# A layer's first DeltaNet unit in another order: substitution ahead of query norm and decay product, masks on VectorE, three weight roundings on ScalarE, gate values in another PSUM bank

## The chip, the cores and the metric

The kernel runs on one core of a Trainium2 chip. The time is that of the whole program on the device, in microseconds (us). TensorE (PE) multiplies matrices into PSUM, VectorE (DVE), ScalarE (ACT) and GpSimd (POOL) work element by element, SyncE (SP) and ScalarE issue the DMA transfers used here. Each engine has one queue of instructions and runs it in order; between engines they wait on semaphores.

## What is computed

Two layers of a hybrid decoder trunk on a sequence of 1024 tokens, width 1024. Each layer projects the normalised input with one matrix of 9232 columns and feeds two branches: a retention branch (4 heads) and a gated DeltaNet branch (8 heads). The change is in the second one.

```python
def gated_deltanet(q, k, v, beta, g):            # chunks; k, q l2-normed after conv and SiLU
    gc = jnp.cumsum(g, axis=-1)                  # within a chunk
    decay = jnp.exp(jnp.where(causal, gc[..., :, None] - gc[..., None, :], -jnp.inf))
    L = jnp.where(strict, einsum(k_beta, k) * decay, 0.0)
    a = L + jnp.eye(C)
    sol = triangular_solve(a, [v * beta, k_beta * exp(gc)])   # lower, unit diagonal
    attn = einsum(q, k) * decay
    ...                                          # recurrence over the chunks
```

beta and g come from sixteen narrow columns of the same projection (the gates).

## The kernel before

**Dense products.** Every weight block is 1024 x 128 in float32. To keep precision it is split into a rounded part w_hi and the rest w_lo (the residual); the activations are split likewise, and each of a block's sixteen pieces is three products with 512 columns (lines 746, 748, 750). Blocks alternate between two slots of w_hi and w_lo. One buffer, w_raw, takes the block from memory, so the load of a block (`load_w`, line 570) waits for the residual of the block before it. The rounding is done by VectorE (`split_w`, line 1581) or, in the even and odd units, by ScalarE (`split_hi`, line 1264); the residual by VectorE (`low_w`, line 1587) in a layer's first unit and by GpSimd (line 2230) elsewhere.

**Units.** The DeltaNet work of a layer is cut into units of half a head, 512 tokens, four chunks of 128. While the recurrence of one half runs, the next half is prepared: gram products of the keys (`gram`, TensorE, line 961), their diagonal for the key norm (`diag`, `keys`), the masked decays (`mask`, line 2308 for the lower one and 2310 for the transposed one, both on GpSimd), their exponentials (`dec`, ScalarE, lines 1393 and 1398), the negated L (`nl`, VectorE, line 1891), the inverse of its 16 x 16 diagonal blocks by substitution (`solve`, thirty small VectorE operations, lines 1976 and 1979), its spread into the full matrix (`spread`, line 1986) and three doubling levels (`turn`, `level_v`, `level_x`), in which TensorE makes two groups of products per level (lines 998 or 1002, then 1013, 1015 or 1017) and VectorE copies or multiplies each result (lines 1946 or 1951, then 1959, 1962 or 1965). The queries are transposed and squared (`qt`), summed for their norm (`qe`, lines 1908 to 1914), and the query-key product (`kq`, TensorE line 978) is multiplied by the transposed decays on VectorE (line 1921).

**The diagonal blocks' way.** The substitution needs the diagonal blocks in another layout, and they go through memory: after `nl` they are stored with small transfers (SyncE line 630, in the first unit half of them ScalarE, line 1413), and when all have landed they are loaded (line 638, and ScalarE line 1423, which stands in its queue behind `kc`, a weight load and the evacuation of the V block's first half).

**The first unit.** A layer starts with a unit that has no recurrence beside it, only preparation of head 0's first half (step index 0) and the keys of its second half (index 1), over the pieces of four blocks Q, V, D, R. The order of all engines comes from one list, `unit_schedule(kind)`: 36 slots (`at(n, step)`), two pieces (`fill`) after the steps of each slot, and after the pieces convolution steps (`conv`), `tanh` and `silu`, none or one or two per slot. Each engine walks the list and issues its own part of each step. In the first unit the substitution starts in slot 17 and the spread is in slot 24. Ahead of the unit TensorE transposes the gate values into bank 3 (line 903), VectorE copies them (line 1752), and from them a chain over both engines makes g_tok (line 1762), the input of the cumulative sum (`gc`, line 941). Gram 0 writes bank 3 as well, and waits for that copy.

## Time and profile before

| | |
|---|---|
| median of 3 runs | 2701.21 us (2700.89 to 2704.86) |
| profiled execution | 2703.87 us, its span 2702.1 us |
| TensorE busy | 98% of the span |
| VectorE, ScalarE, GpSimd busy | 61%, 23%, 31% |
| mean granted TensorE clock | 0.998 |

The profile is one execution. A row of the timeline gives the start in us from the span's start, the time, engine, line and operation, and in brackets how long the engine was idle before it and what released it. Times of matrix products overlap, since they are pipelined. Many tiles of the kernel lie in one tensor called arena, so lines tell more than names.

### The profile page before, as it was taken

To read this page: it belongs to the slowest core of one execution; us is meant where nothing else is said; L and a number is where in the kernel's file an instruction comes from. 1 tells how busy PE (TensorE), PEld (TensorE's weight loads), DVE (VectorE), ACT (ScalarE), POOL (GpSimd) and SP (SyncE) were. 2 spreads that over 40 slices of the span, in tenths; PEclk is the share of its full clock that TensorE was granted. 3 is DMA by queue.
4 is the path that set the end of the run, shared out by engine and by line. 5 is a ranking of instruction groups with operands and counts; after the bars stand their busy time and mean duration, and the time that the engine had idled before them with its cause. 6 is when DMAs were issued, how large, how long until landed. Compare 5 with 4: busy or idle time off the path is not lost.

```text
span 2702.1 us, 39281 instructions
## 1 busy us (share of the span) xinstructions
PE 2654.9 (98%) x14674; PEld 2260.2 (84%) x14674; DVE 1647.2 (61%) x3718; ACT 626.2 (23%) x1261; POOL 836.1 (31%) x459
## 2 busy tenths in 40 slices
PE   7999999999999999999999999999999999999998
PEld 6888888888888888888878888888888888888886
DVE  7878777877744443434587778777877434443333
ACT  5333333333211101200142333333322111120001
POOL 3233333333321212434522333333332122232443
PEclk9999999999999999999999999999999999999999
DMA  4321222122211112433532222222222111133344
GB/s 169 95 87 52 84 63 87 52 84 64 83 42 39 48 35 70 124 100 116 157 95 81 74 78 61 74 73 80 60 78 65 42 49 42 40 107 98 94 140 140
DMA packets 292832, 217.79 MB, mean 81 GB/s; under 512 B 31682, under 2 KB 246036, under 8 KB 292388
## 3 DMA queue, kind: packets, MB, share of 16 engines
q1 hardware_dynamic: 254322, 151.21, 19.6%
q10 hardware_dynamic: 38322, 64.07, 7.1%
q8 instruction: 118, 1.93, 0.3%
q14 instruction: 70, 0.57, 0.1%
HBM read 176.37 MB, written 38.86 MB: 80 GB/s over the span
## 4 chain that ended last, share of the span: by engine, by line
PE 85%; DVE 7%; DMA 2%; POOL 2%; issue 2%; ACT 1%; SPq 1%; ACTq 0%; DVEq 0%; POOLq 0%
PE dense_ps L746 21%; PE dense_ps L750 20%; PE dense_ps L748 20%; PE work L729 3%; PE dense_ps L770 2%; PE dense_ps L771 2%; PE dense_ps L772 2%; PE work L1002 1%; DMA arena<-l_scratch 1%; PE work L961 1%; PE work L1039 1%; PE work L978 1%; PE work L1059 1%; PE work L1028 1%; PE work L1052 1%
## 5 line engine op out<-in xcount | busy, mean ns | idle before, releaser
L746 PE MATMUL dense_ps<-act_hi,w_hi 128*128 128x512 f32 x2560 | 1063.6, 415 | 6.2 <-DVE w_lo L2110 2.4
L750 PE MATMUL dense_ps<-act_hi,w_lo 128*128 128x512 f32 x2560 | 1002.5, 392 | 0.0
L748 PE MATMUL dense_ps<-act_lo,w_hi 128*128 128x512 f32 x2560 | 1000.1, 391 | 0.0
L2230 POOL TENSOR_TENSOR w_lo<-w_raw,w_hi 128x1024 fp32r<-128x1024 f32 x164 | 404.7, 2468 | 1072.1 <-ACT w_hi L1264 565.2
L750 PEld LDWEIGHTS dense_ps<-act_hi,w_lo 128*128 128x128 f32 x2560 | 480.6, 188 | 106.3
L746 PEld LDWEIGHTS dense_ps<-act_hi,w_hi 128*128 128x128 f32 x2560 | 482.9, 189 | 91.0 <-DVE w_lo L2110 2.9
L748 PEld LDWEIGHTS dense_ps<-act_lo,w_hi 128*128 128x128 f32 x2560 | 483.4, 189 | 81.6 <-issue 0.5
L1726 DVE SCALAR_TENSOR_TENSOR arena<-arena,cols 128x512 f32<-128x512 f32 x288 | 241.3, 838 | 5.1
L1581 DVE CAST w_hi<-w_raw 128x1024 fp32r<-128x1024 f32 x90 | 63.7, 708 | 187.8 <-PE dense_ps L772 112.7
L729 PE MATMUL work<-mk,arena 128*128 128x128 f32 x768 | 113.4, 277 | 13.3 <-issue 7.5
L1740 DVE SCALAR_TENSOR_TENSOR arena<-arena 128x512 f32<-128x512 f32 x96 | 112.8, 1175 | 13.2 <-ACT arena L1270 13.1
L1254 ACT ACTIVATE arena<-dense_ps 128x512 f32<-128x512 f32 x96 | 57.4, 598 | 264.8 <-PE dense_ps L750 264.7
L729 PEld LDWEIGHTS work<-mk,arena 128*128 128x128 f32 x768 | 92.0, 143 | 25.3 <-issue 8.0
L1976 DVE TENSOR_TENSOR arena<-arena 128x60 f32<-128x60 f32 (+14 forms) x480 | 99.9, 208 | 18.6 <-DMA arena<-l_scratch 6.0
L2315 POOL TENSOR_TENSOR arena<-arena,negh 128x4 f32<-128x4 f32 x32 | 40.0, 1250 | 225.6 <-DVE arena L1882 225.6
L771 PE MATMUL dense_ps<-v_later_hi,act_lo 128*128 128x256 f32 x384 | 107.9, 281 | 0.0
L772 PE MATMUL dense_ps<-v_later_lo,act_hi 128*128 128x256 f32 x384 | 107.9, 281 | 0.0
L770 PE MATMUL dense_ps<-v_later_hi,act_hi 128*128 128x256 f32 x384 | 107.8, 281 | 0.0
L1979 DVE TENSOR_TENSOR arena<-arena 128x60 f32<-128x60 f32 (+14 forms) x480 | 92.5, 193 | 16.5
L746 PE MATMUL dense_ps<-o_hi,w_hi 128*128 128x512 f32 x256 | 99.6, 389 | 0.0
L748 PE MATMUL dense_ps<-o_lo,w_hi 128*128 128x512 f32 x256 | 99.6, 389 | 0.0
L750 PE MATMUL dense_ps<-o_hi,w_lo 128*128 128x512 f32 x256 | 99.6, 389 | 0.0
(217 smaller groups left out, 3807.9 us busy)
## 6 DMA issues: line engine op xcount, KB each, us to landing
w_raw<-in_w_in SPq DMA_DIRECT2D x138, 512.0 KB, 3.8
gate_scratch<-arena ACTq DMA_DIRECT2D x64, 256.0 KB, 2.3
arena<-gate_scratch ACTq DMA_DIRECT2D x64, 256.0 KB, 3.2
arena<-l_scratch SPq DMA_DIRECT2D x62, 256.0 KB
w_raw<-in_w_out SPq DMA_DIRECT2D x18, 512.0 KB, 4.2
o_scratch<-arena ACTq DMA_DIRECT2D x32, 256.0 KB, 2.0
arena<-o_scratch ACTq DMA_DIRECT2D x32, 256.0 KB, 3.6
w_raw<-in_w_up_dn SPq DMA_DIRECT2D x16, 512.0 KB, 4.2
```

Of the source, the lines that this page charges most:

```text
L729: mm = eng.transpose(wk[bank][:, c * P:(c + 1) * P], src, ident)
L746: eng.matmul(dense_ps[:, to, :], w_hi[:, slot, k, :], hi[:, k, seg], start=(k == 0), stop=False)
L748: eng.matmul(dense_ps[:, to, :], w_hi[:, slot, k, :], lo[:, k, seg], start=False, stop=False)
L750: mm = eng.matmul(dense_ps[:, to, :], w_lo[:, slot, k, :], hi[:, k, seg], start=False, stop=(k == KT - 1))
L770: eng.matmul(dst, act_hi[:, k, tok], hi[:, k, :], start=(k == 0), stop=False)
L771: eng.matmul(dst, act_lo[:, k, tok], hi[:, k, :], start=False, stop=False)
L772: mm = eng.matmul(dst, act_hi[:, k, tok], lo[:, k, :], start=False, stop=(k == KT - 1))
L1726: eng.scalar_tensor_tensor(out=acc[:, i % 2, :], in0=src, scalar=wcol, in1=acc[:, i % 2, :], op0=ALU.mult, op1=ALU.add).then_inc(conv_s.se ...
L1740: eng.scalar_tensor_tensor(out=kqv[:, i // 2, i % 2 * HALF:(i % 2 + 1) * HALF], in0=th[:, i % 2, :], scalar=1.0, in1=acc[:, i % 2, :], op0 ...
L1976: eng.tensor_tensor(xm[:, :, 0:left], column, xs[:, :, k:k + 1].to_broadcast([P, CPH, left]), ALU.mult).then_inc(sv_s.sem, 1)
L1979: eng.tensor_tensor(xs[:, :, k + 1:BASE], xs[:, :, k + 1:BASE], xm[:, :, 0:left], ALU.add)\
L2230: eng.tensor_tensor(w_lo[:, slot, :, :], w_from[second][:, :, :], w_hi[:, slot, :, :].bitcast(F32), ALU.subtract)\
```

## The change

The first unit's list is reordered. The substitution starts in slot 16 and the spread is in slot 22, each level moves with it; the query norm `qe` and the multiplication by the decays (now `kq_decay`) move from slots 15 and 16 behind the spread; the product `kq` itself goes to slot 17. The lower and the transposed mask of both halves are made by VectorE (`mask`, and for the second half `mask_t` apart), no longer by GpSimd. Blocks 1, 2 and 3 of the unit's splits are rounded on ScalarE, and their residuals become steps of their own (`low`) on VectorE, in slots 10, 22 and 31. The gate values are transposed into bank 1 instead of bank 3, and gram 0 no longer waits for their copy.

```diff
-        at(6, "mask", 0)
-        at(8, "dec", 0)
+        at(8, "split", 1)
+        at(9, "mask", 0)
+        at(9, "dec", 0)
         at(10, "nl", 0)
+        at(10, "low", 1)
...
-        at(15, "qe")
-        at(16, "kq")
-        slots[15].insert(0, ("mask", 1))
-        at(19, "dec", 1)
-        solve, spread_at, vt = 17, 24, 34
+        at(17, "kq")
+        at(18, "split", 2)
+        at(25, "dec", 1)
+        at(27, "split", 3)
+        at(31, "low", 3)
+        solve, spread_at, vt = 16, 22, 34
...
         at(spread_at, "spread")
+        if first:
+            at(spread_at, "turn", 0)
+            at(spread_at, "low", 2)
         for n in range(NLV):
             if first or n:
-                at(spread_at + 1 + 3 * n, "turn", n)
+                if n:
+                    at(spread_at + 1 + 3 * n, "turn", n)
                 at(spread_at + 1 + 3 * n, "level_v", n)
                 at(spread_at + 3 + 3 * n, "level_x", n)
+                if first and n == 0:
+                    at(spread_at + 1, "mask", 1)
+                    at(spread_at + 1, "qe")
+                    at(spread_at + 2, "kq_decay")
+                    at(spread_at + 2, "mask_t", 1)
...
-                    mm = eng.matmul(wk[3][:, 16 * c:16 * c + 16], ba[:, c * P:(c + 1) * P], mk[0:32, C_E:C_E + 16],
+                    mm = eng.matmul(wk[1][:, 16 * c:16 * c + 16], ba[:, c * P:(c + 1) * P], mk[0:32, C_E:C_E + 16],
...
-                            if t is None and d == 0:
-                                eng.wait_ge(b_dve.sem, b_dve.after(l, 1))
...
-                        elif what == "split" and kind in ("even", "odd"):
+                        elif what == "split" and (kind in ("even", "odd") or kind == "first" and step[1]):
...
-                eng.tensor_copy(btk, wk[3][:, 0:P].rearrange("p (c n) -> p c n", c=NCH)).then_inc(b_dve.sem, 1)
+                eng.tensor_copy(btk, wk[1][:, 0:P].rearrange("p (c n) -> p c n", c=NCH)).then_inc(b_dve.sem, 1)
...
+                        elif what == "low":
+                            idx = g0 + step[1] + 1
+                            low_w(g + idx, idx % 2)
+                        elif what == "mask" and kind == "first":
+                            w = tn + step[1]
+                            eng.wait_ge(row_in.sem, row_in.after(w, 16))
+                            eng.tensor_tensor(decl[(nb + step[1]) % 2], bcast4(mk[:, C_NL:C_NL + P]), chunk_rows,
+                                              ALU.subtract).then_inc(m_ok.sem, 1)
+                            if step[1] == 0:
+                                eng.tensor_tensor(dect, chunk_rows, bcast4(mk[:, C_NT:C_NT + P]), ALU.add)\
+                                   .then_inc(m_ok.sem, 1)
+                        elif what == "mask_t":
+                            w = tn + step[1]
+                            eng.wait_ge(row_in.sem, row_in.after(w, 16))
+                            eng.wait_ge(aT_ok.sem, aT_ok.after(w, 0))
+                            eng.tensor_tensor(dect, chunk_rows, bcast4(mk[:, C_NT:C_NT + P]), ALU.add)\
+                               .then_inc(m_ok.sem, 1)
```

The order in which the new list has VectorE work behind the spread: transpose 0, residual of block 2, two convolution steps, result of the first product of level 0 (line 1946), mask of the second half, query norm, two convolution steps, multiplication by the decays, transposed mask, one SiLU, a convolution step, result of the second product of level 0 (line 1959), diagonal of gram 1, two convolution steps, transposes 1, first result of level 1, key operations, negated L of the second half, a SiLU, second result of level 1. TensorE has two pieces between slots, so it issues the first product of level 0 (line 998) after 46 pieces instead of 50.

## Rows read from the trace of the kernel before

**Rows 1.** The page: busy times; a group of VectorE's instructions

```profile
PE 2654.9 (98%) x14674; PEld 2260.2 (84%) x14674; DVE 1647.2 (61%) x3718; ACT 626.2 (23%) x1261; POOL 836.1 (31%) x459
...
L1726 DVE SCALAR_TENSOR_TENSOR arena<-arena,cols 128x512 f32<-128x512 f32 x288 | 241.3, 838 | 5.1
```

**Rows 2.** Waits of TensorE, whole run: us in total, times, longest

```profile
PE work L1015 <- DVE arena L1951: 3.1, 2, 1.6
...
PE work L998 <- DVE arena L1986: 1.9, 2, 1.0
...
PE work L978 <- ACT arena L1437: 0.3, 1, 0.3
```

**Rows 3.** TensorE in order of time, first unit of layer 0

```profile
46.93 1.16 PE L961 MATMUL work<-arena 128*128 128x128 f32 x8 [0.46 <-DVE arena L1752]
...
50.70 0.33 PE L941 MATMUL work<-g_tok,mk 128*128 128x64 f32 x2
...
85.34 0.39 PE L748 MATMUL dense_ps<-act_lo,w_hi 128*128 128x512 f32 x1
85.57 0.39 PE L750 MATMUL dense_ps<-act_hi,w_lo 128*128 128x512 f32 x1
87.00 1.00 PE L998 MATMUL work<-arena 128*112 128x64 f32 x8 [1.04 <-DVE arena L1986]
...
93.51 0.39 PE L750 MATMUL dense_ps<-act_hi,w_lo 128*128 128x512 f32 x1
94.04 0.89 PE L1002 MATMUL work<-arena 128*96 128x64 f32 x8
...
99.29 0.66 PE L1015 MATMUL work<-arena 112*66 112x64 f32 x8 [1.55 <-DVE arena L1951]
```

**Rows 4.** The same of layer 1

```profile
1377.02 2.05 PE L961 MATMUL work<-arena 128*128 128x128 f32 x8 [0.45 <-DVE arena L1752]
...
1382.37 0.33 PE L941 MATMUL work<-g_tok,mk 128*128 128x64 f32 x2
...
1417.96 1.00 PE L998 MATMUL work<-arena 128*112 128x64 f32 x8 [0.88 <-DVE arena L1986]
```

**Rows 5.** Windows: busy us of PE, PEld, DVE, ACT, POOL, clock, DMA, GB/s

```profile
77.00:78.00 1.00, 1.00 (x6) 0.84 (x5) 1.00 (x1) 0.42 (x2) 0.54 (x1) 1.00 0.00 0
1378.00:1379.00 1.00, 1.00 (x7) 1.00 (x6) 0.00 (x0) 0.98 (x2) 0.00 (x0) 0.50 0.86 209
90.00:100.00 10.00, 8.31 (x51) 6.58 (x50) 9.63 (x24) 1.23 (x2) 1.40 (x1) 1.00 0.21 57
```

**Rows 6.** VectorE in order of time, first unit of layer 0

```profile
50.02 0.22 DVE L1762 SCALAR_TENSOR_TENSOR g_tok<-arena,abias 128x64 f32<-128x64 f32 x1
...
61.30 1.22 DVE L1587 TENSOR_TENSOR w_lo<-w_raw,w_hi 128x1024 fp32r<-128x1024 f32 x1
62.45 1.80 DVE L1726 SCALAR_TENSOR_TENSOR arena<-arena,cols 128x512 f32<-128x512 f32 x1
...
79.21 0.25 DVE L1976 TENSOR_TENSOR arena<-arena 128x60 f32<-128x60 f32 x1
...
86.25 0.69 DVE L1986 TENSOR_TENSOR arena<-arena,mk 128x512 f32<-128x512 f32 x1
...
93.57 0.41 DVE L1959 TENSOR_TENSOR arena<-arena,work 112x256 f32<-112x256 f32 x1
...
98.72 0.42 DVE L1951 COPY arena<-work 96x256 f32<-96x256 f32 x1
```

**Rows 7.** GpSimd in order of time, the same stretch

```profile
62.26 1.45 POOL L2308 TENSOR_TENSOR arena<-mk,arena 128x512 f32<-128x512 f32 x1 [2.72 <-DMA arena<-row_scratch]
```

**Rows 8.** ScalarE and its queue of transfers, the same stretch

```profile
65.44 1.28 ACT L1398 ACTIVATE arena<-arena 128x128 f32<-128x128 f32 x4 [0.36 <-POOL arena L2310]
...
71.07 0.68 ACTq L1423 DMA_DIRECT2D arena<-l_scratch  x1
```

**Rows 9.** SyncE's queue of transfers, the same stretch

```profile
101.54 1.22 SPq L638 DMA_DIRECT2D arena<-l_scratch  x2
```

More of the change, by code:

```diff
@@ L216, in unit_schedule @@
                 break
-            if pieces % (2 * KT) == 0 and (pieces or kind not in ("first", "odd_last")):
+            if pieces % (2 * KT) == 0 and not first and (pieces or kind != "odd_last"):
                 step = ("split", pieces // (2 * KT))
-                if first and step[1] == 3:
-                    ropes.append((n + 3, step))
-                else:
-                    waiting.insert(0, step)
+                waiting.insert(0, step)
                 if kind == "even_last" and step[1] == 2:
@@ L1815, in delta_unit @@
                     ns_of = slice(CPH * nb, CPH * nb + CPH)
+                    chunk_rows = gcb.rearrange("p (c t) -> p c t", c=CPH)
                     for step in unit_schedule(kind):
@@ L1837, in delta_unit @@
                                 split_v(l, 0, idx - BLK_RET - 2)
-                            elif kind not in ("even", "odd"):
+                            elif kind not in ("even", "odd", "first"):
                                 eng.wait_ge(w_hi_ok.sem, w_hi_ok.after(g + idx, 0))
                                 split_w(g + idx, idx % 2)
-                            if kind == "first":
+                            elif kind == "first" and step[1] == 0:
+                                split_w(g + idx, idx % 2)
                                 low_w(g + idx, idx % 2)
+                        elif what == "low":
[15 more added lines that the diff above has]
+                               .then_inc(m_ok.sem, 1)
                         elif what == "conv":
@@ L1915, in delta_unit @@
                                .then_inc(qe_s.sem, 1)
-                        elif what == "kq":
+                        elif what == ("kq_decay" if kind == "first" else "kq"):
                             eng.wait_ge(kq_ps.sem, kq_ps.after(tn, 1))
@@ L2302, in delta_unit @@
                                 split_w(g + idx, idx % 2)
-                        elif what == "mask":
+                        elif what == "mask" and kind != "first":
                             w = tn + step[1]
```

## The prediction

> **What bounds the kernel now.** I read the page first: TensorE is busy 98% of the span [rows 1], so only a stretch in which it waits can be shortened, and only new waits can lengthen it. Next the waits of TensorE over the whole run: the products of the inverse (L998, L1015) and the query-key product (L978) waited 1.9, 3.1 and 0.3 us [rows 2]. Then TensorE in order of time in the first unit of layer 0 [rows 3]. Dense products start every 0.23 us (85.34, 85.57) and are shown as 0.39 long, so a wait costs its idle time and 0.16 more. Gram 0 loses 0.46 + 0.16 = 0.62, L978 0.26 + 0.16 = 0.42, L998 1.04 + 0.16 = 1.20 (87.00 instead of 85.80), L1015 1.55 + 0.16 = 1.71. L1002 starts at 94.04 instead of 93.74, the slot after 93.51: 0.30. That is 4.2 us. In layer 1 gram 0 loses 0.61 and L998 1.04 [rows 4], L1015 as much as in layer 0 (3.1 in two times, [rows 2]), L1002 is taken at the same 0.30, and L978 waited once only, in layer 0: 3.7 us. There the clock also falls: granted 0.50 of full speed, the 1.2 GHz level, around 1378 [rows 5]. From gram 0 to the cumulative sum takes 5.35 us there against 3.77 in layer 0 (1377.02 to 1382.37, 46.93 to 50.70) [rows 3, 4], so the dip costs 1.6 us. All of what the change can win is therefore 4.2 + 3.7 + 1.6 = 9.5 us.
>
> **What the sum is made against.** The profiled execution took 2703.87 us (span 2702.1 and 1.8 around it), the median of the runs is 2701.21 and they spread over 4 us. I add the difference to the median. A measurement of this kernel can tell about 0.2%, 5.4 us, from no change.
>
> **Gate bank.** TensorE waits before gram 0 for VectorE's copy of the gate values, because both use one bank. With bank 1 for the gates gram 0 starts at 46.31. The chain behind the copy is not moved, it ends in g_tok at 50.24 [rows 6], and the cumulative sum, now due at 50.70 - 0.62 = 50.08 [rows 3], waits for it: the gain is 0.4, not 0.62.
>
> **Masks on VectorE.** Four masks of 128x512 per layer leave GpSimd. The first mask began there at 62.26, when the row of decays had landed [rows 7]. On VectorE an operation of that shape is taken at 0.6 a piece: the spread at 86.25 has 0.69 [rows 6], and I let 0.08 of each hide behind the next, as the 0.39 of a dense product does behind 0.23. So VectorE gets 2.4 us of work, and loses the collisions: L1726 took 1.80 at 62.45, while GpSimd worked, against 0.84 in the mean of the kernel [rows 1, 6, 7]; an estimate, four such collisions per layer, is some 4 us. I price this as freed time ahead of the substitution, and as 1.2 us added after it, where the second pair of masks now stands. What gets earlier is the decay: the second exponential waited for GpSimd until 65.44; with the masks done at 62.9 and 63.5 and the first four exponentials in 1.3 it can start at about 64.2 [rows 8]. ScalarE's stores of the diagonal blocks and its load of them (71.07) stand behind it in its queue, and come 1.3 earlier: the load goes out at about 69.7. It can hardly be earlier: the evacuation of the V block's first half, which waits for TensorE, stands ahead of it in the queue.
>
> **Three roundings on ScalarE.** ScalarE is little used; its rounding is not on a path as long as each stands well ahead of the residual on VectorE. Each removes a cast from VectorE, priced at 0.7, the 0.69 of one operand's full pass like the spread's [rows 6]. One of the three would have stood ahead of the substitution where VectorE will now idle, one behind it; the residual of the same block stays (1.15 to the next start, 61.30 to 62.45) and moves behind the spread and the first transpose. It feeds the load of the next block, a queue further on, and that block is wanted 16 pieces, 11 us, later, against a landing of about 5: covered. If that cover went, TensorE would wait at L746.
>
> **Substitution first.** It needs the blocks loaded. Before, the DMA engines were silent from 77.0 on [rows 5], so the load issued at 71.07 was there by 77.0, 5.9 us later, and the substitution began at 79.21 without waiting for it [rows 6]. Issued at 69.7 it is there at 75.6. VectorE is free well before (query norm, decay product and cast no longer stand ahead), about 73, and now waits for the DMA. How the load's landing moves is not shown: between 73 (VectorE is ready, no wait) and 77.0 (it does not move). I take 75.6, by its issue row. The substitution then starts 3.55 earlier than at 79.21, and L998, which follows 7.79 after its start (79.21 to 87.00), can start at 83.4. But the schedule also asks for it four pieces (2.73 us) sooner. TensorE is there at 85.80 - 2.73 - 0.4 (gate bank) - 0.41 (the query-key product is two pieces later, its squares are done) = 82.3. **Wait 1.1**, against 1.20 before.
>
> **Behind the substitution** I use the old stretch as a meter. From the start of the spread to the end of L1959 (86.25 to 93.98) VectorE took 7.73 [rows 6]. In the new order this stretch gains the residual 1.15, a mask 0.6, clearing, sum and scaling for the query norm 1.1 (one full operation at 0.6, and 0.5 for two small ones, each between the 0.25 of a substitution step and a full one), the decay product 0.6 and the second mask 0.6: 4.05. It loses the mask and sum of gram 1 (0.6 + 0.7) and four small key operations (taken at 0.55, at 0.25 or less each as a substitution step [rows 6], partly in a row): 1.85. The convolution steps are five in either. So it lasts 9.93, and L1002 comes about 9.2 after L998. TensorE needs 7.04 - 0.30 = 6.74 for what lies between (87.00 to 94.04, less its wait; six pieces and gram 1 in either order). **Wait 2.5**, where it was 0.30. From L1959 to the copy at 98.72 to 99.14 it was 5.16, with the four products of the negated L (1.04), a cast and a residual (1.85) and one step in it; these leave, gram 1's mask and sum (1.3) and another step (0.75) enter: about 4.4. TensorE needs 3.55 (0.70 and four pieces): **wait 0.9** instead of 1.70. Then key operations, negated L, one SiLU and two copies stand ahead of the third level, about 2.8, where TensorE needs 1.95 for L1015 and two pieces: **wait 0.9** instead of none. The last residual is then beside four pieces, hidden.
>
> **Sum.** New waits 0.2 + 1.1 + 2.5 + 0.9 + 0.9 = 5.6 us per layer. Layer 0: 5.6 - 4.2 = +1.4. Layer 1: 5.6 - 3.7 = +1.9, the dip counted as it was. Together +3.3: **2704.5 us**, 0.12% over the median. Bounds: with the load there at 73 everything is 2.4 earlier per layer, -1.5 in all, and -3.1 if the dip goes with its wait: 2698. With the load unmoved at 77.0, 1.4 later per layer: 2707.3, and with a dip more 2709.
>
> **Moved behind the unit.** The negated L of the second half moves from about 95 to 98.6. Its stores and load are on SyncE's queue: the load was issued at 101.54 [rows 9] and would be at about 105. The next block's weight load stands behind it there, and waits for a later residual anyway. The next substitution began at 110.05 before, the load needs 5.9 or more, and rope and Z transfers of the same time share the engines. So it may be late by 0 to 1.3 us on TensorE. I take 0, since everything behind the unit is 1.4 later too, and keep 1.3 for the range. The Z block's load goes out behind the last residual, some 4 us later; its rounding stands in ScalarE's queue ahead of the copies of the next unit's recurrence, with about 1 us to spare by the same count.
>
> **Rivals.** (a) *The second half's blocks come late* and the load of the first half does not move: 1.3 + 1.4 per layer over the forecast, 3.3 + 5.4 = +8.7, 2710. It decides once the first half's load lands after 76.8 and the second's after about 112. For it: stores and loads in a chain on one queue, with rope's transfer beside. Against: the DMA was silent for two microseconds before the first substitution. Chance with its milder forms beyond 5.4 us: 0.14. (b) *The clock falls in a new wait.* From 90 to 100 us TensorE was busy 8.31 and the granted clock stayed at 1.00; at 1378, behind the narrow gate products (L903) and a wait, it was 0.50 [rows 5]. A wait of 2.5 with two of 0.9 behind it is more than the trace has in one place at full clock. Each dip costs 1.6 by the row above; in both layers, on top of the forecast, +6.5: 2707.7. Chance 0.10. The Trainium skill (TensorE: Matmul & The Clock Gate, section on oscillation) says that waits between bursts of products can bring the array's clock back to half; by that rule this case is the likelier, the 90 to 100 row speaks against it. (c) *The waits go*: the load lands early and VectorE, rid of collisions and casts, keeps ahead: 2701.2 - 9.5 = 2691.7. For it: VectorE's total falls by some 3.5 us a layer. Against: what falls lies ahead of the substitution, where it becomes idle time, and the added 2.2 us lie between spread and L1002. Chance 0.08. (d) *It does nothing that shows*, early landing with half the forecast's waits, or the dip gone: 2698 to 2702, 0.18. The forecast itself, 2702 to 2706.6: 0.50.
>
> **How the numbers follow.** Faster by over 0.2%: (c), 0.08. Slower by over 0.2%: (a) and most of (b), 0.22. Same: 0.70. The range runs from the early load without a dip, 2698.0, to the late load with one dip, 2709.0; outside it are (c) and the far end of (a).
>
> **What would show it.** Right: VectorE idle before L1976 for the DMA of the blocks, from about 73 to 75.6; TensorE waiting for L1959's result some 2 us or more before the second level; no wait before gram 0; GpSimd without masks near 62 and 74, and L1726 at 0.75 there. Wrong: L998 without a wait, or L1002 waiting under 1 us (my account of the stretch is off), or waits of TensorE in the units behind, or a granted clock of 0.50 near 90.

## The result, and the profile of the kernel after

After takes 2709.68 us (median of 10 runs, 2707.43 to 2713.29), before takes 2704.25 us in 10 runs, of which the prediction had seen three. The ratio is 1.0023, with a 95% interval of 1.0013 to 1.0032: slower by 0.23%. The profiled execution took 2710.29 us (span 2708.5, granted clock 0.997); that of before 2703.87. The three runs that the prediction started from had a median 1.5 to 3 us below those of the five larger sets of before taken in this study (2702.75 to 2704.25). In the ratio the forecast, 2704.5 on 2701.21, was 1.0012. So the sign was right and the size was not: +3.3 us forecast, +5.4 measured by the two medians (the interval of the ratio is 3.5 to 8.7 us).

The busy times on the page of after, which answer to [rows 1]:

```profile
PE 2655.6 (98%) x14674; PEld 2260.6 (83%) x14674; DVE 1641.3 (61%) x3720; ACT 632.1 (23%) x1267; POOL 822.7 (30%) x451
...
L1733 DVE SCALAR_TENSOR_TENSOR arena<-arena,cols 128x512 f32<-128x512 f32 x288 | 240.3, 834 | 5.1
```

GpSimd lost 13.4 us and VectorE 5.9 us of work, ScalarE gained 5.9, and none of it shows in the time. TensorE is busy as long as it was (2655.6 against 2654.9). The time is in its waits, shown here over the whole run (us in total, times, longest), as in [rows 2]:

```profile
PE work L1035 <- DVE arena L2036: 3.7, 2, 2.9
PE work L1009 <- DVE arena L1985: 3.5, 2, 2.4
PE work L1005 <- DVE arena L2012: 3.2, 2, 1.7
...
PE work L1022 <- DVE arena L1977: 1.5, 2, 0.8
```

L1005 is before's L998 (inverse products), L1009 its L1002 and L1022 its L1015 (the levels). L1035 is before's L1028, a product of the *next* unit's recurrence, which waited 0.8 in two times there. Both of its waits in after are in layer 0: 2.88 at 120.48 and 0.83 at 749.96, in a much later unit; behind layer 1's first unit it did not wait. TensorE in order of time in layer 0, as in [rows 3]:

```profile
46.20 1.05 PE L968 MATMUL work<-arena 128*128 128x128 f32 x8
50.20 0.43 PE L950 MATMUL work<-g_tok,mk 128*128 128x64 f32 x2 [0.18 <-DVE g_tok L1769]
...
83.98 1.00 PE L1005 MATMUL work<-arena 128*112 128x64 f32 x8 [1.66 <-DVE arena L2012]
...
93.46 0.89 PE L1009 MATMUL work<-arena 128*96 128x64 f32 x8 [2.44 <-DVE arena L1985]
97.92 0.66 PE L1022 MATMUL work<-arena 112*66 112x64 f32 x8 [0.77 <-DVE arena L1977]
100.77 0.69 PE L1009 MATMUL work<-arena 128*66 128x64 f32 x8 [0.73 <-DVE arena L1989]
...
120.48 0.77 PE L1035 MATMUL work<-arena 128*128 128x128 f32 x2 [2.88 <-DVE arena L2036]
120.90 0.77 PE L755 MATMUL dense_ps<-act_hi,w_hi 128*128 128x512 f32 x1
121.47 0.63 PE L757 MATMUL dense_ps<-act_lo,w_hi 128*128 128x512 f32 x1
```

and in layer 1, as in [rows 4]:

```profile
1422.68 1.00 PE L1005 MATMUL work<-arena 128*112 128x64 f32 x8 [1.55 <-DVE arena L2012]
...
1432.17 0.89 PE L1009 MATMUL work<-arena 128*96 128x64 f32 x8 [1.01 <-DVE arena L1985]
```

VectorE in layer 0, as in [rows 6]: the first mask, the idle time ahead of the substitution, the spread, L1985 (before's L1959), and then the second half:

```profile
61.90 0.69 DVE L1858 TENSOR_TENSOR arena<-mk,arena 128x512 f32<-128x512 f32 x1 [1.08 <-DMA arena<-row_scratch]
...
76.17 0.26 DVE L2002 TENSOR_TENSOR arena<-arena 128x60 f32<-128x60 f32 x1 [4.09 <-DMA arena<-l_scratch]
...
83.23 0.69 DVE L2012 TENSOR_TENSOR arena<-arena,mk 128x512 f32<-128x512 f32 x1
...
92.99 0.42 DVE L1985 TENSOR_TENSOR arena<-arena,work 112x256 f32<-112x256 f32 x1
...
97.35 0.42 DVE L1977 COPY arena<-work 96x256 f32<-96x256 f32 x1
...
116.93 0.26 DVE L2002 TENSOR_TENSOR arena<-arena 128x60 f32<-128x60 f32 x1 [4.41 <-DMA arena<-l_scratch]
...
119.99 0.35 DVE L2036 SCALAR_TENSOR_TENSOR arena<-arena,work 128x128 f32<-128x128 f32 x1
```

The last two lines are the surprise. VectorE stood 4.41 us for the second half's blocks, with the recurrence's state update (L2036) queued behind the first steps of that substitution; so TensorE, which needs the state, stood 2.88 at L1035. The two queues of transfers, as in [rows 8] and [rows 9] (start, issue time, then what):

```profile
69.50 0.69 ACTq L1430 DMA_DIRECT2D arena<-l_scratch  x1
...
103.08 0.39 ACTq L1374 DMA_DIRECT2D w_raw<-in_w_in  x1
...
107.30 0.44 ACTq L1463 DMA_DIRECT2D arena<-in_rope  x1
```

```profile
99.65 4.93 SPq L639 DMA_DIRECT2D l_scratch<-arena  x8
107.25 1.22 SPq L647 DMA_DIRECT2D arena<-l_scratch  x2
```

The second half's load goes out at 107.25 (before 101.54) and is there at 116.9, 9.7 us later; before it was there by 110.05, at most 8.5 us later. It goes out once the eight stores have landed. Six of them took 1.3 to 1.8 us, the last two, with the Z block's load under way (103.08 to 107.07), 3.08 and 4.42. In layer 1 of the same execution all eight took under 1.5, the load went out at 1443.00, 3 us ahead of the rope table's (1446.02), and VectorE did not wait for it:

```profile
1438.36 3.60 SPq L639 DMA_DIRECT2D l_scratch<-arena  x8
1443.00 1.22 SPq L647 DMA_DIRECT2D arena<-l_scratch  x2
```

Windows of after, columns as in [rows 5]:

```profile
90.00:100.00 10.00, 6.79 (x39) 4.87 (x37) 9.62 (x25) 5.86 (x14) 1.01 (x1) 1.00 0.07 26
...
113.00:116.00 3.00, 3.00 (x22) 2.67 (x20) 0.00 (x0) 1.36 (x3) 0.00 (x0) 1.00 1.03 269
116.00:119.00 3.00, 1.60 (x8) 1.00 (x7) 1.83 (x8) 0.00 (x0) 0.00 (x0) 1.00 0.39 113
119.00:122.00 3.00, 1.52 (x5) 1.36 (x6) 2.69 (x13) 0.00 (x0) 0.00 (x0) 0.68 0.00 0
122.00:125.00 3.00, 3.00 (x17) 2.62 (x16) 1.79 (x10) 0.28 (x1) 0.00 (x0) 0.75 0.00 0
```

The DMA engines are full shortly before the landing, and behind the wait the clock is at 0.68 and 0.75 of full speed in the mean, which is a stretch at 1.2 GHz. One sees it in the dense products too: they start 0.43 us apart (121.47, 121.90) instead of 0.23. Below, "a dip" is such a stretch. Each one near a first unit is 3.5 us long and takes 1.7 us of full clock. Before has one at 1377.0, behind gram 0 of layer 1, and after has none there, but one at 120.0 and one at 1423.9, behind L1005.

**Where the time went.** I follow the start of the gram products on TensorE (before's L961, after's L968). The third one of layer 0 starts at 134.12 in before and 6.86 later in after, and that shift stays to the end of the layer's DeltaNet part. Only part of it comes from the unit's own waits: the same dense product behind the third level (104.00 in before) is 2.38 later in after, with no dip so far. The other 4.5 come at L1035 and in the dip behind it. Between the layers the shift grows by 1.8, 1.1 of it in one wait for a residual (1.77 at 1100 us, 0.64 in before). Layer 1's stretch from its first to its third gram product (88.05 in before) is 2.09 longer; counted from ahead of gram 0, whose own wait is gone, 1.50. Some 2.3 us come back at two places in later units of layer 1 (1.4 and 0.9) where before's execution waited for late blocks and after's did not. There the shift is 8.0, and 6.4 at the end of the run.

### The profile page after: what moved, and what is told of

The parts are those of the page before. It is cut to its first block, busy times and chain, and to the rows that moved or that the text cites. A ratio compares the mean times of both kernels' runs of the same rounds, so it can differ in the third digit from the quotient of the medians.

```text
span 2708.5 us, 39279 instructions
## 1 busy us (share of the span) xinstructions
PE 2655.6 (98%) x14674; PEld 2260.6 (83%) x14674; DVE 1641.3 (61%) x3720; ACT 632.1 (23%) x1267; POOL 822.7 (30%) x451
## 4 chain that ended last, share of the span: by engine, by line
PE 87%; DVE 6%; DMA 2%; issue 2%; ACT 1%; POOL 1%; SPq 0%; ACTq 0%; DVEq 0%; POOLq 0%
PE dense_ps L755 21%; PE dense_ps L759 21%; PE dense_ps L757 21%; PE work L738 3%; PE dense_ps L779 2%; PE dense_ps L780 2%; PE dense_ps L781 2%; PE work L1009 1%; DMA arena<-l_scratch 1%; PE work L1046 1%; PE work L1066 1%; PE work L985 1%; PE work L968 1%; PE work L1035 1%; PE work L1059 1%
## 5 line engine op out<-in xcount | busy, mean ns | idle before, releaser
L1733 DVE SCALAR_TENSOR_TENSOR arena<-arena,cols 128x512 f32<-128x512 f32 x288 | 240.3, 834 | 5.1
L1271 ACT ACTIVATE w_hi<-w_raw 128x1024 fp32r<-128x1024 f32 x92 | 96.9, 1053 | 16.8 <-ACT arena L1378 8.0
```

The source lines that it names most:

```text
L1271: eng.activation(w_hi[:, slot, :, :], w_raw[:, :, :], ACT.Copy).then_inc(w_hi_ok.sem, 1)
L1733: eng.scalar_tensor_tensor(out=acc[:, i % 2, :], in0=src, scalar=wcol, in1=acc[:, i % 2, :], op0=ALU.mult, op1=ALU.add).then_inc(conv_s.se ...
```

## The experiments

Each kernel was run in five rounds against before. The table has the ratio to before, then from the one profiled execution of each: how much later than in before the third gram product of layer 0 starts; the same for layer 1's stretch between first and third; and what the clock cost in the first unit of layer 0 and layer 1, worked out from windows of 5 us as 5 x (1 - granted clock). That last number comes in steps of 1.7 us, one for each dip. Two kernels differ clearly only if their intervals of about 0.09% (2.5 us) to either side are apart.

| kernel | median, us | ratio to before (95%) | layer 0 | layer 1 | clock |
|---|---|---|---|---|---|
| before | 2702.8 to 2704.3 | 1 | 0 | 0 | 0 / 1.7 |
| after | 2709.68 | 1.0023 (1.0013 to 1.0032) | +6.86 | +2.09 | 1.7 / 1.7 |
| e1_fill | 2707.98 | 1.0014 (1.0005 to 1.0023) | +5.68 | +0.49 | 3.4 / 0 |
| e2_masks_back | 2710.59 | 1.0023 (1.0014 to 1.0033) | +3.28 | +2.59 | 1.7 / 3.4 |
| e3_rope_late | 2709.77 | 1.0024 (1.0015 to 1.0033) | +2.57 | +2.10 | 1.7 / 1.7 |
| e4_bank_only | 2702.35 | 0.9993 (0.9984 to 1.0002) | -0.48 | -0.40 | 0 / 0 |
| e5_fill_rope | 2702.90 | 1.0000 (0.9991 to 1.0009) | +0.69 | -0.25 | 0 / 1.7 |
| e6_fill_rope_23 | 2700.32 | 0.9993 (0.9984 to 1.0002) | -2.19 | -0.45 | 0 / 1.7 |
| e7_order_back | 2707.11 | 1.0015 (1.0006 to 1.0024) | +4.21 | +2.75 | 3.4 / 1.7 |
| e8_round_back | 2711.86 | 1.0035 (1.0023 to 1.0048) | +5.00 | +3.09 | 3.4 / 1.7 |
| e9_order_back2 | 2700.07 | 0.9984 (0.9975 to 0.9993) | -1.50 | -1.72 | 0 / 0 |
| e10_bank_rope | 2703.23 | 0.9997 (0.9988 to 1.0006) | -0.05 | -0.64 | 0 / 0 |
| e11_fill_24 | 2706.26 | 1.0005 (0.9997 to 1.0014) | +1.04 | -0.40 | 1.7 / 0 |
| e12_fill_24_res | 2699.66 | 0.9986 (0.9977 to 0.9995) | -1.94 | -1.67 | 0 / 0 |

**e1_fill: the work from behind the spread put ahead of the substitution.**

```diff
+        at(16, "mask", 1)
+        at(16, "qe")
+        at(17, "kq_decay")
+        at(17, "mask_t", 1)
...
-        at(25, "dec", 1)
+        at(19, "dec", 1)
...
-        solve, spread_at, vt = 16, 22, 34
+        solve, spread_at, vt = 17, 22, 34
...
-                if first and n == 0:
-                    at(spread_at + 1, "mask", 1)
-                    at(spread_at + 1, "qe")
-                    at(spread_at + 2, "kq_decay")
-                    at(spread_at + 2, "mask_t", 1)
```

> The changed kernel with one part of its order taken back: query norm, mask of the second half, decay product and transposed mask stand ahead of the substitution, in the 4 us in which VectorE waits for the diagonal blocks, and the substitution starts one slot later; the spread stays in slot 22, masks on VectorE, roundings on ScalarE and the gate bank stay. Theory A (the cost is what stands behind the spread, 3.9 us with one convolution step): the wait for L1985 (2.4 in layer 0) goes, the waits of the second level and third level fall to under 0.5, the negated L of the second half is about 3.9 us earlier, so the second half's blocks are there before VectorE asks for them and TensorE's 2.9 us at L1035 go as well. The wait at L1005 for the substitution stays at about 1.7. Time 2699 to 2703 us against 2704 of the kernel before and 2710 of the changed one. Rival B (masks or roundings on their new engines are the cost): the time stays near 2710, since they stay where the change put them. Rival C (the early level products are the cost, whatever stands behind): waits of some 2 us remain in the levels and the time is 2706 or more.

The waits of 2.4, 0.8 and 0.7 at the levels went, and VectorE idled 0.64 ahead of the substitution instead of 4.09. But the wait at the inverse products was 2.2 instead of 1.7, with a dip behind it, and the recurrence waited longer, 3.7, for the same reason as in after (1.5 in layer 1 too). TensorE's waits of this kernel from 44 to 126 us:

```profile
PE work L1034 <- DVE arena L2035: 3.7, 1, 3.7
PE work L1004 <- DVE arena L2011: 2.2, 1, 2.2
PE work L949 <- DVE g_tok L1768: 0.2, 1, 0.2
```

The time, 2707.98, is 5 us above theory A's range, and its interval overlaps with after's. It is in rival C's range, but C's waits of some 2 us in the levels did not come. So the long stretch behind the spread makes waits of its own, but taking them away alone gives no clear gain: the load went out at 104.63 and was there at 115.7, 11.1 us later, although the stores ahead of it went out 1.4 us earlier than in after (98.21 against 99.65).

**e2_masks_back: the four masks on GpSimd again**, at after's places.

```diff
-                        elif what == "mask" and kind != "first":
+                        elif what in ("mask", "mask_t"):
```

(with VectorE's own mask steps taken out)

> The changed kernel with all four masks back on GpSimd, in the new places of the list. Theory A: VectorE loses 1.3 us of masks behind the spread, so the wait for L1985 falls from 2.4 to about 1.2 if GpSimd's masks do not collide there, and to no less than about 2 if they do; ahead of the substitution the decay is later by about 1.3 us, since GpSimd takes 1.45 and 1.75 for the pair, and the wait at L1005 grows by about as much. Sum: within 1.5 us of the changed kernel, 2708 to 2711. Rival B (masks on VectorE are the cost): it falls to that of the kernel before, 2704 or lower.

The time does not move (1.0023 both). The wait at the inverse products is 2.7 and 2.5 us instead of 1.7 and 1.6, the second level's 0.7 instead of 2.4: what VectorE gains in one place it loses in the other. Most of the second is the clock's doing, though: a dip behind the inverse products holds TensorE back by 1.7 us there, and VectorE's stretch from the spread to this result is only 0.37 shorter (9.81, 10.18). The time is the same with either engine, so the engine of the masks is not what makes after slow.

**e3_rope_late: the load of the rope table two units later**, behind the first even and odd unit.

```diff
-                eng.wait_ge(b_st.sem, b_st.after(l, 16))
-                eng.dma_start(rope_t, rope.rearrange("p (a t) -> p a t", a=2)).then_inc(rope_in.sem, 16)
...
                     delta_unit("odd", h)
+                    if h == 0:
+                        eng.wait_ge(b_st.sem, b_st.after(l, 16))
+                        eng.dma_start(rope_t, rope.rearrange("p (a t) -> p a t", a=2)).then_inc(rope_in.sem, 16)
```

> The changed kernel with the 1 MB load of the rope table issued two units later (it is read only some 650 us later). Theory D (the second half's blocks are late, since their load shares the engines of the DMA with the rope table and the Z block): the load, 9.7 us in the changed kernel's profile, takes about 6, and TensorE's wait at L1035 (2.9 and 0.8 us) goes or falls under 0.5; the first unit's own waits (1.7, 2.4, 0.8, 0.7) stay. Time 2705 to 2708. Rival E (they are late because the negated L and its stores are late, whatever shares the DMA): the wait stays at 2 us or more in layer 0 and the time within 1 us of the changed kernel.

In the profile the late blocks are gone: the load issued at 104.47 is in use at 112.61, VectorE does not wait for it, and L1035 does not wait in either layer. Not all of that is the rope table's: the load also goes out 2.8 us sooner than in after, since the last two stores took 1.44 and 1.45 this time, and the table's own load comes behind these stores in after as well (107.30). SyncE's queue, two windows around the fall of the clock (columns as in [rows 5]), and TensorE's waits, 44 to 126 us:

```profile
99.83 3.60 SPq L639 DMA_DIRECT2D l_scratch<-arena  x8
104.47 1.22 SPq L647 DMA_DIRECT2D arena<-l_scratch  x2
...
90.00:95.00 5.00, 2.55 (x15) 1.99 (x13) 4.86 (x10) 3.80 (x11) 0.00 (x0) 0.86 0.00 0
95.00:100.00 5.00, 5.00 (x25) 4.09 (x24) 4.76 (x16) 2.18 (x3) 1.01 (x1) 0.80 0.00 0
...
PE work L1009 <- DVE arena L1986: 2.4, 1, 2.4
PE work L1005 <- DVE arena L2013: 1.8, 1, 1.8
PE work L950 <- DVE g_tok L1770: 0.2, 1, 0.2
```

Yet the median is that of after, and 1.8 us above the expected range. So the late second half in after's profile (2.9 us of wait and the dip behind it) is real in that execution, but the two intervals hardly leave room for it in every execution. The number of dips is the same, only their place is not: here the dip follows the wait of 2.4, the same wait behind which after's clock had stayed up. And it costs almost nothing there. The waits of 0.77 and 0.73 at the later levels are gone, and the dense product behind the third level is 2.58 later than in before, against 2.38 in after, which had no dip so far. TensorE, slower for 3.5 us, arrives when VectorE is ready.

**e4_bank_only: before with the gate bank alone.**

```diff
-                            if t is None and d == 0:
-                                eng.wait_ge(b_dve.sem, b_dve.after(l, 1))
...
-                    mm = eng.matmul(wk[3][:, 16 * c:16 * c + 16], ba[:, c * P:(c + 1) * P], mk[0:32, C_E:C_E + 16],
+                    mm = eng.matmul(wk[1][:, 16 * c:16 * c + 16], ba[:, c * P:(c + 1) * P], mk[0:32, C_E:C_E + 16],
```

> The kernel before with the gate bank alone: gate values in bank 1, no wait ahead of gram 0. My account: gram 0 loses its 0.6, the cumulative sum takes 0.2 of it back, so 0.4 per layer, 0.8 us in all, and the dip of the clock at 1378 may go with it (1.6). Time 2702 to 2704 against 2704. Rival: whatever TensorE gains is waited for at L998, since the substitution is bound by the blocks' load, whose issue follows TensorE: no difference beyond 0.3 us.

(The copy reads bank 1 too.) About 1 us better than before in the medians, within the interval. Layer 0 gains 0.48 by its third gram product, with a wait of 0.2 for g_tok, against a forecast of 0.4. In layer 1 the dip behind gram 0 is gone with its wait, and yet, counted from ahead of gram 0, the layer gains only 1.0 us: TensorE now waits 1.26 instead of 0.88 at the inverse products, and 0.24 more at the query-key product.

**e5_fill_rope: e1 and e3 together.**

> After, with both earlier edits together: the second masks, query norm, decay product and second exponential ahead of the substitution (its start a slot later), and the rope table's load sent one unit later. Theory C (two causes: the long stretch of VectorE between spread and second level, and the second half's blocks landing late because their load of 9.7 to 11 us shares the DMA engines with the rope table and the Z block): both waits are gone in both layers, no wait over 0.5 us at the second level's product and none at the recurrence behind the unit; the second half's load lands within 7 us of its issue. What is left is the wait before the first inverse product (2.2 and 1.4). The time is then within 1 us of the kernel with the gate bank alone (2702.4), some 2702 to 2704. Rival D (the late blocks come from something else, the order of SyncE's queue): a recurrence wait of over 1.5 us stays in layer 0, and the time is 2706 to 2708. Rival E (waits of TensorE don't tell the time; what they save comes back as dips of the clock): 2708 or more.

2702.90, a ratio of 1.0000, as theory C said. Two edits that saved 0.09% and nothing by themselves, both within the noise, save 0.23% together. In the profiles each had left the other's wait, and a dip, standing; whether the two together give more than their sum, the intervals don't tell. One comparison is clear: e5 differs from e3 by the order alone, the same four steps and the second exponential ahead of the substitution (its start a slot later), and is 0.24% faster, with the intervals apart (0.9991 to 1.0009, 1.0015 to 1.0033). Rival E, that waits don't tell the time, is out by its number, and so is D, but for a remainder that theory C had at nothing: in layer 0 the load still took 8.5 us (102.89 to 111.44, VectorE idle 2.65, L1034 waiting 1.1), and only in layer 1 was it down to 6.1.

**e6_fill_rope_23: the spread one slot later**, on top of e5.

```diff
-        solve, spread_at, vt = 17, 22, 34
+        solve, spread_at, vt = 17, 23, 34
```

> The same with the spread, and with it the inverse products and levels, one slot (two pieces, 1.4 us) later on TensorE; the substitution's place on VectorE is unchanged. Theory C: the first inverse product's wait of 2.2 and 1.4 falls to 0.8 and 0, and nothing else is late, since the vt product has room: 1 to 1.5 us per layer below the kernel without this step, some 2700 to 2702, which would be below before. If instead the level chain becomes late by the same slot, waits move to the levels' last products and the time is as in the kernel without this step. Rival E: no difference between the two.

In the expected range: 2700.32, the wait at the inverse products 0.3 and 0.55 instead of 1.9 and 2.4, with one of 0.85 for the third block's residual behind it in each layer. The intervals of e5 and e6 overlap, and that of e6 includes before. After had moved the spread two slots ahead of before's, and that asked for it sooner than the chain could give it.

**e7_order_back: after with before's order of steps**; masks stay on VectorE, roundings on ScalarE, gates in bank 1.

```diff
+        at(6, "mask", 0)
+        at(8, "dec", 0)
         at(8, "split", 1)
-        at(9, "mask", 0)
-        at(9, "dec", 0)
...
-        at(17, "kq")
-        at(18, "split", 2)
-        at(25, "dec", 1)
+        at(15, "mask", 1)
+        at(15, "qe")
+        at(16, "kq")
+        at(16, "kq_decay")
+        at(16, "mask_t", 1)
+        at(16, "split", 2)
+        at(17, "low", 2)
+        at(19, "dec", 1)
         at(27, "split", 3)
         at(31, "low", 3)
-        solve, spread_at, vt = 16, 22, 34
+        solve, spread_at, vt = 17, 24, 34
...
```

(The steps that after has at and behind the spread go too, and transpose 0 is back in the slot behind it.)

> After with the old order of the first unit: first masks, query norm and decay product ahead of the substitution, spread and levels at their old slots; masks stay on VectorE, the three roundings on ScalarE (the residual of each a slot or more behind), gates in bank 1. Theory F (the order alone makes the kernel slower, because VectorE stands idle ahead of the substitution and the work comes behind it): the second level waits under 1 us, no recurrence wait, and the time is that of the gate bank alone, 2701 to 2704. Rival G (masks on VectorE and the roundings cost too): 2705 to 2708, with a wait at the first inverse product above the 1.0 to 1.3 it has with the gate bank alone.

2707.11: by its number the rival's. The profile says something else. The second level's product never waits; what waits is the recurrence, for ScalarE (3.44 us in layer 0, 3.47 in layer 1). TensorE and ScalarE in order of time, and ScalarE's queue:

```profile
108.66 0.80 PE L1055 MATMUL work<-arena 128*128 128x128 f32 x2 [3.44 <-ACT arena L1445]
```

```profile
99.87 0.39 ACTq L1370 DMA_DIRECT2D w_raw<-in_w_in  x1
...
107.39 1.06 ACT L1267 ACTIVATE w_hi<-w_raw 128x1024 fp32r<-128x1024 f32 x1 [4.22 <-DMA w_raw<-in_w_in]
108.35 0.26 ACT L1445 ACTIVATE arena<-work 128x128 f32<-128x128 f32 x1
```

The Z block's load went out at 99.87 (before 97.58), because it waits for the last residual, which stands four slots behind its rounding (27 and 31). It landed 7.5 us later; its rounding on ScalarE waited 4.22 for it, and the copy of the state (L1445) stood behind the rounding. The blocks' load had gone out beside it, at 99.58. In after the Z load had landed before the blocks' went out (103.08 to 107.07, 107.25) and its rounding found the weights there at 107.95, without a wait.

**e9_order_back2: the same with that residual in the slot behind its rounding.**

```diff
-        at(31, "low", 3)
+        at(28, "low", 3)
```

> The old order again, with one step mended: the residual of the last block right behind its rounding instead of three slots later. In the first try the load of the Z block, which waits for that residual, landed 7.5 us after its issue, and ScalarE, which rounds that block ahead of copying the recurrence's state, stood with it: TensorE waited 3.5 us in each layer. Theory F (the order alone makes the kernel slower): with that wait gone the kernel is within 1 us of the one with the gate bank alone: 2701.5 to 2703.5, and no wait of TensorE over 1.5 us in the first unit. Rival G (masks and roundings on the other engines cost time in the old order too): 2705 or more.

2700.07, a ratio of 0.9984 (0.9975 to 0.9993): the wait and all dips of the first units gone, 0.31% below e7 and 0.39% below after, and 1.4 us below theory F's own range. G falls. F, that the order alone makes the kernel slower, is borne out with a reservation: between after and e9 the place of the last residual changed too, and after with that step alone was not run. In after's profile nothing waited for the state copy, so the step had no wait to mend there; but e7, the old order without it, is not clearly faster than after (1.0006 to 1.0024 against 1.0013 to 1.0032). TensorE's waits, 44 to 126 us:

```profile
PE work L1018 <- DVE arena L1973: 0.8, 1, 0.8
PE work L1001 <- DVE arena L2008: 0.6, 1, 0.6
PE work L734 <- DVE arena L1743: 0.4, 1, 0.4
PE work L946 <- DVE g_tok L1765: 0.2, 1, 0.2
PE work L1005 <- DVE arena L1981: 0.2, 1, 0.2
```

All parts of the change except its order (and this slot) are in this kernel, and of those shown here it is the first that beats before by more than its interval. Whether masks and roundings help beside the gate bank (0.9993, up to 1.0002) the two intervals, which overlap, don't tell.

**e8_round_back: the three roundings on VectorE again**, in after.

```diff
-                        elif what == "split" and (kind in ("even", "odd") or kind == "first" and step[1]):
+                        elif what == "split" and kind in ("even", "odd"):
```

(and the cast ahead of each residual on VectorE)

> After with the three roundings back on VectorE, each right ahead of its residual; all else as in after. By the price of the prediction VectorE gets three casts of 0.7 us: one where it is idle ahead of the substitution (free), one right behind the spread, one beside the last level. The second level's product then waits 2.4 + 0.7 = 3.1 in layer 0 and 1.7 in layer 1, and the time is 1.4 to 2 us above after (2709.7), some 2711. Rival: the cast is hidden where the residual waits for its weights anyway, and the time is that of after within 0.5.

2711.86, 2.2 above after's median; the interval overlaps with after's. The wait at the second level is 1.7 and 2.4 us, not 3.1 and 1.7, the recurrence waits 1.2 for ScalarE's state copy in layer 0, and two dips stand there. The size came out near the forecast, by other terms.

**e10_bank_rope: before with gate bank and late rope table.**

> Before, with the gate bank and the rope table's load one unit later, nothing else. In before the second half's load was there in time, so by theory C the later rope table gives nothing: the time of the gate bank alone, 2701.5 to 2703. Rival: the transfer costs something in before too, in the weight load beside it, and the time falls by 1 us or more, below 2701.

0.9997 against 0.9993 for the gate bank alone: nothing, as expected. In before the rope table's load goes out 2.9 us behind the second half's (101.54, 104.43), and moving it gives nothing.

**e11_fill_24 and e12_fill_24_res: the spread at before's slot 24**, the third block's residual ahead of it; in e12 the last residual at slot 28 as in e9.

```diff
+        at(22, "low", 2)
-        solve, spread_at, vt = 17, 23, 34
+        solve, spread_at, vt = 17, 24, 34
-            at(spread_at, "low", 2)
```

(against e6)

> The best version so far (second masks, query norm, decay product and second exponential ahead of the substitution, rope table late, spread at slot 23) with the spread one slot later still, at the old slot 24, and the residual of the third block ahead of the spread. That version still waited in each layer 0.3 and 0.5 us before the first inverse product and 0.85 us for the residual right behind it. Expected: both gone, 1.2 us per layer, 2697.5 to 2699.5, faster than before by over 0.1%. Rival: the residual makes the spread later by more than the slot gives, the wait before the first inverse product is 0.5 us or more, and the time that of the version without this step, 2700 to 2701.

> The version with the spread at slot 24 and the third block's residual ahead of it, with the last block's residual right behind its rounding (slot 28 instead of 31), the same mend as in the old order. Theory: as there, the wait of the recurrence for ScalarE's state copy (5.2 us in two times) goes; no wait over 1 us is left in the first units; the time falls by 5 to 8 us, from 2706.3 to 2698 to 2701, level with or below the mended old order (2700.1). Rival: the rounding itself at slot 27 with its weight load beside the stores is what holds ScalarE, and a wait of over 1.5 us stays.

e11 took 2706.26, neither of the two cases. The waits at the inverse products were gone and 0.5 to 0.8 was left for the residual, but the state copy was late by 2.5 and 2.7 us, the wait of e7 again: the blocks' load now went out at 98.10 and the Z weights' at 98.55, beside it, and took 6.6 us, where in e6 it had gone out at 99.52, ahead of the blocks (102.03), and taken 4.0. With the last residual three slots earlier, e12 takes 2699.66 (0.9986, 0.9977 to 0.9995). Its time is in the expected range and the state copy's wait is gone, but one wait above 1 us is left, 1.4 for the third block's residual in layer 1. TensorE's waits of e12 in layer 1, 1374 to 1466 us:

```profile
PE dense_ps L754 <- DVE w_lo L1594: 1.4, 1, 1.4
PE work L1021 <- DVE arena L1977: 0.8, 1, 0.8
PE work L949 <- DVE g_tok L1769: 0.2, 1, 0.2
```

e9 and e12 are the best versions; they can't be told apart.

## Why the prediction was wrong in its size

**Right, with sizes.** Gram 0 started at 46.20 (forecast 46.31), g_tok cost 0.2, the load of the blocks went out at 69.50 (69.7), landed at 76.1 (75.6), and the substitution waited for it. The masks took 0.7 us each on VectorE, and three L1733 in a row took 2.32 at 58.50, so the 1.80 of [rows 6] went with GpSimd's masks. VectorE's total fell by 2.95 us a layer (3.5). L1005 came 7.81 behind the substitution's start, as the 7.79 of before said. Spread to the end of L1985 took 10.18 (83.23 to 93.41; forecast 9.93), and from there to the end of the copy at 97.77 it was 4.36 (4.4).

**The base.** The sum was added to 2701.21, the median of three runs; the ten runs have 2704.25. That is 3.0 of the 5.2 us between the forecast of 2704.5 and the 2709.68 measured, and no step of the mechanism. The change itself makes the other 2.1.

**The first unit's own waits, term by term.** The prediction counts 0.16 with each idle time. With it the five waits of layer 0 are 0.34, 1.82, 2.60, 0.93 and 0.89, together 6.6 us where the sum had 5.6. Most of that is "Wait 1.1": the load of the blocks took 6.6 us from issue instead of 5.9, and TensorE was there a little sooner, so L1005 lost 1.8. Layer 0 is 2.4 us later behind the levels, not 1.4. Layer 1 is 1.5 later, not 1.9. The term "the dip counted as it was" was right by luck: before's dip went with gram 0's wait, as in e4, and another came behind L1005. Together the first units cost 3.9 us in after's profile, and 4.1 in e3's, against 3.3.

**The step that failed is "Moved behind the unit", which the sum took at 0.** The reason given was that all that follows is later too. The load of the second half's blocks went out not 3.5 but 5.7 us later than in before (107.25, 101.54), behind two stores that took 3.08 and 4.42, and took 9.7 us where I had 5.9 or more: it ran beside the rope table, issued at 107.30, and the next weight block, issued at 111.48. TensorE waited 2.88 behind a state update that stands in VectorE's queue behind the substitution. That path, queue order on VectorE, was in no rival. With the dip that followed it this is 4.5 of layer 0's 6.86 us. It happened in layer 0 only, and e3, whose profile is free of it, has after's median; so how much of it a median execution has stays open. The Trainium skill (DMA: Bandwidth & Descriptors, section "Issuing engines are not separate DMA queues") says that transfers issued by different engines share the same DMA engines. The trace agrees: the share is 1.03 from 113 to 116 us, with transfers of SyncE and ScalarE under way.

**Rival (b), the clock,** had a chance of 0.10 and nothing in the sum for layer 0. Layer 0 has a dip in after, and in every kernel with after's order (e2, e3 and e8 too, e8 with two). It is not one profile's accident: the mean granted clock noted for each run, times the span, makes 8.4 us lost to the clock over the ten runs of after, 8.6 over e3's eleven and 6.7 over the hundred of before in the experiments (noted to 0.001, so a mean over many runs only). The 1.7 between them is one dip more. What a dip adds to the time is not shown, though. Behind a late wait it adds most of its 1.7; within the levels it takes the place of waits, 0.2 in all in e3. So the 2.1 us that the change cost beyond the forecast can't be split: 0.6 to 0.8 are in the first units, the rest is in late blocks and dips that come in some executions, and the interval of the ratio (3.5 to 8.7 us) is wider than it. The row of 90 to 100 us at clock 1.00, on which I set the chance, had 8.31 us of PE busy; after has 6.79 there and also kept 1.00, and then lost the clock behind the next wait. The Trainium skill (TensorE: Matmul & The Clock Gate, section on oscillation) says that waits between bursts of products can bring the clock to half; the traces agree, the dips in these units stand behind waits, but which wait brings one they do not show.

**Rival (a)** named the late blocks with a chance of 0.14 and a price of 1.3 a layer; they came in one layer of one execution, at 2.88. **Rival (c)** fails on the idle time that it named itself: VectorE's freed time became 4.09 us of waiting ahead of the substitution. The range ended at 2709.0, 0.7 us short; the low base is more than that.

## What to carry to other kernels

Moving a chain ahead of its neighbours pays only if what it starts from arrives earlier too: here the substitution waited 4 us for its blocks, and the displaced work came back behind it, where TensorE waits for VectorE. The old order with the same engine assignments, and one residual mended, was 0.39% faster than the new. Before moving a weight rounding to another engine, follow its load back to what frees the buffer: a residual that stood three slots later cost 0.31% and 0.19% (e7 against e9, e11 against e12), through a copy that only stood behind the rounding in ScalarE's queue. And two edits that save little alone may each leave the other's wait standing, as e1 and e3 did in their profiles: try them together before dropping them.

## What the runs showed of the hardware

A dip takes 1.7 us of full clock here, and less of the time where TensorE would have waited anyway: 0.2 in e3's layer 0. The wait ahead of it doesn't tell whether it comes: none behind 2.44 us in after or 1.86 in e5 (layer 0), one behind 2.4 in e3, one behind 0.55 and 0.86 in e6 (layer 1). Of the six kernels with no wait over 1.6 us in the first units, four had no dip there (e4, e9, e10, e12), e6 had that one, and before had one, at a gram 0 that had waited 0.45. The same load of blocks (two transfers of 256 KB) took from at most 5.8 us (e6, 102.03 to 107.84) to 11.1 us (e1), by what else was under way, and the 512 KB of the Z block's weights from 3.7 (e1) to 7.5 us (e7). A store of 4 KB took 1.45 us in e3 and up to 4.42 in after, at the same place of the program. In how many runs of after the second half comes late is open: each kernel has one profile, and no run here shows the spread of that wait.
